# The norm of the heads: an inverse root with a Newton step instead of a root and a reciprocal

## The reference

```python
mu = jnp.mean(o, axis=-1, keepdims=True)                       # over the 64 channels of a head
var = jnp.mean(jnp.square(o - mu), axis=-1, keepdims=True)
o = (o - mu) * lax.rsqrt(var + GN_EPS) * lnx_w + lnx_b
bonus = sum over directions of (sum over channels of r * k_dir * r_k) * v
o = (o + bonus) * g                                            # g = sigmoid(gd) @ g_up
y_rwkv = o @ w_o_rwkv
```

## Time and profile before

| | |
|---|---|
| time, median of 3 runs | 2914.91 us (2911.87 to 2917.02) |
| the profiled execution's own time | 2906.37 us |
| its span | 2904.6 us |
| `head_norm`, first load to its last operation | about 1732 to 1806 us |
| TensorE, VectorE, ScalarE, GpSimd busy | 95%, 62%, 34%, 20% of the span |

### The profile page before, as it was taken

How to read it: one execution, slowest core, us unless ns; L and a number is a source line. 1 busy time by engine, 2 the same in 40 slices (tenths; PEclk the granted TensorE clock), 3 DMA queues, 4 the chain that set the end, 5 groups by cost and what they waited for, 6 DMA issues and landing times. The chain is left out here.

```text
span 2904.6 us, 58716 instructions
## 1 busy us (share of the span) xinstructions
PE 2760.1 (95%) x23048; PEld 2632.4 (91%) x23048; DVE 1799.9 (62%) x3391; ACT 995.6 (34%) x1768; POOL 575.7 (20%) x721
## 2 busy tenths in 40 slices
PE   7999999999999999999799987999899999999998
PEld 4999999999998999999788865799899999899998
DVE  4455565556636446434477858454777777777776
ACT  4211111111114323443266645212444443443442
POOL 4112233333203101222243314122300000100000
PEclk9999999999999999999899998999999999999999
DMA  6225556665511433344744423321243443344442
GB/s 277 66 79 142 153 154 166 173 157 147 141 40 72 142 126 113 140 167 174 211 104 112 108 63 144 127 78 62 94 128 126 136 134 123 110 131 135 137 134 94
DMA packets 246581, 371.75 MB, mean 128 GB/s; under 512 B 106528, under 2 KB 145824, under 8 KB 244032
## 3 DMA queue, kind: packets, MB, share of 16 engines
q1 hardware_dynamic: 213952, 295.45, 31.0%
q0 software_dynamic: 30208, 73.62, 10.3%
q10 hardware_dynamic: 2240, 0.13, 0.0%
HBM read 314.00 MB, written 101.25 MB: 143 GB/s over the span
## 5 line engine op out<-in xcount | busy, mean ns | idle before, releaser
L1788 PE MATMUL bank<-right_hi_ffn,left_lo_ffn 128*128 128x288 f32 x1240 | 368.4, 297 | 16.4 <-DVE u_ffn L1566 5.2
L1788 PE MATMUL bank<-right_lo_ffn,left_hi_ffn 128*128 128x288 f32 x1240 | 366.8, 296 | 0.0
L1788 PE MATMUL bank<-right_hi_ffn,left_hi_ffn 128*128 128x288 f32 x1240 | 365.8, 295 | 0.0
L917 DVE SCALAR_TENSOR_TENSOR x<-bank,gate,x 128x128 f32<-128x128 f32 (+1 forms) x480 | 235.9, 514 | 114.1 <-PE bank L1047 113.6
L2532 PE MATMUL bank<-h_hi_mix,wlo_in 128*128 128x384 f32 x840 | 288.6, 344 | 1.8 <-DVE h_lo_mix L242 1.8
L2532 PE MATMUL bank<-h_lo_mix,whi_in 128*128 128x384 f32 x840 | 282.5, 336 | 0.0
L2532 PE MATMUL bank<-h_hi_mix,whi_in 128*128 128x384 f32 x840 | 282.4, 336 | 0.0
L1353 ACT ACTIVATE left_hi_ffn<-raw_ffn 128x512 fp32r<-128x512 f32 x302 | 188.1, 626 | 225.3 <-PE bank L1788 219.2
L1546 DVE SCALAR_TENSOR_TENSOR x<-bank,gate,x 128x288 f32<-128x288 f32 (+2 forms) x440 | 190.1, 452 | 110.5 <-PE bank L1823 108.7
L1788 PEld LDWEIGHTS bank<-right_hi_ffn,left_lo_ffn 128*128 128x128 f32 x1240 | 234.3, 189 | 18.9 <-issue 17.7
L1102 ACT ACTIVATE act_out_ffn<-bank 128x384 f32<-128x384 f32 x66 | 32.4, 491 | 623.8 <-PE bank L1018 623.8
(11 more groups left out here) (357 smaller groups left out, 6893.6 us busy)
## 6 DMA issues: line engine op xcount, KB each, us to landing
raw_ffn<-tile_sums SPq DMA_DIRECT2D x168, 256.0 KB, 2.7
raw_ffn<-in_ffn_w SPq DMA_DIRECT2D x134, 256.0 KB, 2.9
raw_d_ffn<-in_ffn_w SPq DMA_DIRECT2D x66, 512.0 KB, 4.8
tile_sums<-in_ffn_w POOLq DMA_DIRECT2D x132, 256.0 KB, 7.1
ada_beside_ffn<-in_ada_w POOLq DMA_DIRECT2D x96, 256.0 KB, 3.5
raw_in<-in_w_in SPq DMA_DIRECT2D x35, 512.0 KB, 5.0
mix<-row_out SPq DMA_DIRECT2D x23, 576.0 KB, 3.2
raw_a_ffn<-in_ffn_w SPq DMA_DIRECT2D x22, 512.0 KB, 5.8
```

The lines of the kernel that those rows point to most:

```text
L917: ins = nc.vector.scalar_tensor_tensor(xs, kit.banks[4 + d % 4][:, a:b], kit.gate[:, gate, d, cond:cond + 1], xs, ALU.mult, ALU.add)
L1788: mm = nc.tensor.matmul(out, w[:, j, cols], v[:, r, k], start=(opens and a == 0 and k == 0 and m == 0), stop=(a == len(terms) - 1 and k == ...
```

## The change

The root becomes an inverse root (`Abs_reciprocal_sqrt`) on ScalarE, which also squares it. VectorE then does one Newton step in three products instead of a reciprocal and a product: with y the inverse root and V the sum of squares, (V + 64 eps) * y^2, minus 3*64, times y, and that times the centered tile and lnx_w * (-0.5/64), which is computed once. lnx_b is added in the product with the gate, since the gate's product is where the whole sum is multiplied. Squares and roots get two small buffers of their own (two slots each) instead of `hn_r`, so `square` no longer waits for `weighted`. TensorE's order becomes variance (1), sums (0), bonus (1), gate (2), channels (4); ScalarE's root (1), square (0), channels and high (4); VectorE's center (0), normed (1), bonus (1), gated (3); GpSimd's weighted (0), with_bonus (4), low (5).

```diff
         def tensor(pe):
             def sums(m):
                 if m >= 2:
-                    pe.wait_ge(s["rooted"], m - 1)
+                    pe.wait_ge(s["stepped"], m - 1)
...
-                nc.tensor.matmul(bank(m, 0), cst.pair_ones, at(r, m), start=True, stop=True).then_inc(s["var_done"], 1)
+                nc.tensor.matmul(bank(m, 0), cst.pair_ones, square_at(m), start=True, stop=True).then_inc(s["var_done"], 1)
...
-            skewed([(0, sums), (1, bonus), (1, variance), (2, gate), (3, channels)])
+            skewed([(1, variance), (0, sums), (1, bonus), (2, gate), (4, channels)])
...
                 act.wait_ge(s["centered"], m + 1)
-                act.wait_ge(s["rk_ready"], m + 1)
-                nc.scalar.activation(at(r, m), at(o, m), ACT.Square).then_inc(s["squared"], 1)
+                nc.scalar.activation(square_at(m), at(o, m), ACT.Square).then_inc(s["squared"], 1)
...
-                nc.scalar.activation(at(r, m), bank(m, 0), ACT.Sqrt, scale=1.0 / HD, bias=kit.eps[:, 1:2])\
-                    .then_inc(s["rooted"], 1)
-
-            def affine(m):
-                act.wait_ge(s["scaled"], m + 1)
-                nc.scalar.activation(at(r, m), at(o, m), ACT.Identity, scale=kit.col("lnx_w", ct_of(m)),
-                                     bias=kit.col("lnx_b", ct_of(m))).then_inc(s["affine"], 1)
+                nc.scalar.activation(root_at(m), bank(m, 0), ACT.Abs_reciprocal_sqrt, scale=1.0 / HD,
+                                     bias=kit.eps[:, 1:2]).then_inc(s["rooted"], 1)
+                act.wait_ge(s["rooted"], m + 1)
+                nc.scalar.activation(square_at(m), root_at(m), ACT.Square).then_inc(s["root_squared"], 1)
...
-            skewed([(0, square), (1, root), (2, affine), (3, channels), (3, high)])
+            skewed([(1, root), (0, square), (4, channels), (4, high)])
...
-                dve.wait_ge(s["rooted"], m + 1)
-                nc.vector.reciprocal(at(kd_sum, m), at(r, m)).then_inc(s["inverted"], 1)
+                dve.wait_ge(s["root_squared"], m + 1)
+                nc.vector.scalar_tensor_tensor(square_at(m), bank(m, 0), HD * GN_EPS, square_at(m), ALU.add, ALU.mult)\
+                    .then_inc(s["stepped"], 1)
+                dve.wait_ge(s["stepped"], m + 1)
+                nc.vector.scalar_tensor_tensor(root_at(m), square_at(m), 3.0 * HD, root_at(m), ALU.subtract, ALU.mult)\
+                    .then_inc(s["inverted"], 1)
                 dve.wait_ge(s["inverted"], m + 1)
-                nc.vector.tensor_tensor(at(o, m), at(o, m), at(kd_sum, m), ALU.mult).then_inc(s["scaled"], 1)
+                nc.vector.scalar_tensor_tensor(at(o, m), at(o, m), scale[:, ct_of(m):ct_of(m) + 1], root_at(m), ALU.mult, ALU.mult)\
+                    .then_inc(s["scaled"], 1)
...
-                nc.vector.tensor_tensor(at(o, m), bank(m, 2), at(v, m), ALU.mult).then_inc(s["gated"], 1)
-            skewed([(0, center), (2, bonus), (3, gated), (1, normed)])
+                nc.vector.scalar_tensor_tensor(at(o, m), at(v, m), kit.col("lnx_b", ct_of(m)), bank(m, 2), ALU.add, ALU.mult)\
+                    .then_inc(s["gated"], 1)
+            nc.vector.tensor_scalar(scale[:], kit.col("lnx_w", 0, CT), -0.5 / HD, None, ALU.mult).then_inc(s["weights"], 1)
+            skewed([(0, center), (1, normed), (1, bonus), (3, gated)])
...
-                pool.wait_ge(s["affine"], m + 1)
+                pool.wait_ge(s["scaled"], m + 1)
...
-                nc.gpsimd.tensor_tensor(at(v, m), at(v, m), at(r, m), ALU.add).then_inc(s["with_bonus"], 1)
+                nc.gpsimd.tensor_tensor(at(v, m), at(v, m), at(o, m), ALU.add).then_inc(s["with_bonus"], 1)
...
-            skewed([(0, weighted), (2, with_bonus), (3, low)])
+            skewed([(0, weighted), (4, with_bonus), (5, low)])
```

More of the change, by code:

```diff
@@ L3188, in head_norm @@
     s = {q: kit.sem("hn_" + q) for q in (
-        "loaded", "mean_done", "centered", "rk_ones", "rk_ready", "squared", "var_done", "rooted", "inverted", "scaled",
-        "affine", "bonus_done", "bonus_v", "with_bonus", "gate_done", "gated", "hi_ready", "lo_ready",
+        "loaded", "mean_done", "centered", "rk_ones", "rk_ready", "squared", "var_done", "rooted", "root_squared",
+        "stepped", "inverted", "scaled", "weights", "bonus_done", "bonus_v", "with_bonus", "gate_done", "gated", "hi_ready", "lo_ready",
         "f_in", "dft_in", "g_done", "g_ready")}
@@ L3199, in head_norm @@
         f, cs = buf("fo_f", [P, FG, T]), buf("fo_cs", [P, 2 * FD])
-        one_root = buf("hn_one_root", [P, 1])
+        one_root, scale = buf("hn_one_root", [P, 1]), buf("hn_scale", [P, CT])
+        squares, roots = buf("hn_squares", [P, 2, CH]), buf("hn_roots", [P, 2, CH])
         steps = CT * NC
@@ L3203, in head_norm @@
         at = lambda a, m: a[:, ct_of(m), part(m)]
+        square_at, root_at = (lambda m: squares[:, m % 2]), (lambda m: roots[:, m % 2])
         bank = lambda m, q: kit.banks[4 * (m % 2) + q][:, 0:CH]
@@ L3316, in channels @@
                 ins.then_inc(s["g_ready"], 1)
-            nc.scalar.activation(one_root[:], kit.eps[:, 0:1], ACT.Sqrt)
-            skewed([(0, square), (1, root), (2, affine), (3, channels), (3, high)])
+            nc.scalar.activation(one_root[:], kit.eps[:, 0:1], ACT.Abs_reciprocal_sqrt)
+            skewed([(1, root), (0, square), (4, channels), (4, high)])
         def vector(dve):
@@ L3327, in normed @@
             def normed(m):
[L3328 to L3329 removed]
+                dve.wait_ge(s["root_squared"], m + 1)
[4 more added lines that the diff above has]
+                    .then_inc(s["inverted"], 1)
                 dve.wait_ge(s["inverted"], m + 1)
[L3331 removed]
+                if m == 0:
+                    dve.wait_ge(s["weights"], 1)
+                nc.vector.scalar_tensor_tensor(at(o, m), at(o, m), scale[:, ct_of(m):ct_of(m) + 1], root_at(m), ALU.mult, ALU.mult)\
+                    .then_inc(s["scaled"], 1)
             def bonus(m):
@@ L3423, in tensor @@
                 if q < 3:
-                    pe.wait_ge(prev.s[("rooted", "bonus_v", "gated")[q]], prev.steps)
+                    pe.wait_ge(prev.s[("stepped", "bonus_v", "gated")[q]], prev.steps)
                 for i in range(4):
```

## The result

The changed kernel took 2893.4 us in the median of 6 runs (2887.14 to 2901.43), the kernel before 2913.39 (6 runs, 2908.27 to 2917.02): ratio 0.994, 95% interval 0.9926 to 0.9954, that is 13 to 22 us less, 17.5 in the middle (the two medians lie 20.0 apart). Timed again on another occasion it gave 0.9941 (0.9927 to 0.9955). The forecast was 2899.8, a gain of 15.1, with 2891 to 2908 as its range.

The account below looks back on a forecast made before the run. The prediction took VectorE, with its long reciprocal, to bound the stage at 5.5 us per tile. Start and period -15.3, tail +0.95 and clock -0.8 gave -15.1 us: 2899.8 from the median 2914.91, range 2891 to 2908.

Parts of the forecast that it names:

- VectorE's round and the port: VectorE's work per tile 3.13 us instead of 5.50; with port waits behind GpSimd, period 4.0, bounds 3.75 and 5.0.
- Rival 1: Both new VectorE products always wait a whole GpSimd product: period 5.0, gain 8.6, 2906.3 us; chance 17%.
- TensorE's floor of 3.75: TensorE's own work per tile in the stage, 3.75 us, taken as the shortest possible period.
- the second loop of the prediction: Loop from center through high and GpSimd's low, weighted and with_bonus to gated: 6.6 to 8.1 us for two periods.
- The start: DMA of `f` stays the wait; center(5) at 1753.7, then six periods of 4.0: center(11) 15.3 us earlier.
- The tail: From center(11) to the context transform, later lags of channels and low cost 0.95 us.
- The clock: TensorE's context transform runs at full clock: -0.8 us; the extra columns behind it taken as 0.
- Rival 4: TensorE's clock holds through the extra columns too: up to 5 us more gain, 2895; chance 11%.
- The table: ScalarE's next-stage Sqrt at 2056.83 will need a table load: 0, at most 1.3 us.
- rival 2: Inverse root and Square lie in different ScalarE tables, two loads per tile: gain about 7, 2908 us; chance 4%.
- Rival 3: TensorE's clock halves in the stage and stays there: 7.3 us per round, +5, 2920 us; chance 3%.
- The sum: Start and period -15.3, tail +0.95, clock -0.8: -15.1 us in all, giving 2899.8 us.

Follow-up runs that it names:

- e4: The changed kernel with the results of stepped and inverted written to PSUM instead of SBUF; median 2890.34 us, 0.9934 of the kernel before.
- e3: The changed kernel with GpSimd's with_bonus at lag 2 and low at 3 instead of 4 and 5; one execution 2905.57 us, kernel before beside it 2913.30.
- e2: The kernel before with the new order of all engines but the old arithmetic; one execution 2904.13 us, kernel before beside it 2913.30.
- e9: e4 with the 16 context transform products put among the 32 products of 2 columns; one execution 2890.72 us, kernel before beside it 2902.64.
- e6: The kernel before with idle matrix products in two holes of TensorE's tail; one execution 2910.45 us, kernel before beside it 2914.30.
- e8: The changed kernel with GpSimd's with_bonus at lag 2 and low at 4; one execution 2885.75 us, kernel before beside it 2902.64.
- e5: The changed kernel with TensorE's context transform made to wait for GpSimd's last product; one execution 2905.19 us, kernel before beside it 2914.30.

## Why the prediction was right, step by step

- **VectorE's round and the port**: 3.13 us plus waits, period 4.0; measured 3.96, and `inverted` and `scaled` 0.21 us each over their length in e4, 0.42 in all against 0.3 taken. The forecast had `inverted` alone wait; in the trace it differs from tile to tile, and `scaled` is held whole (1.24 against 0.62) in four of twelve. Rival 1 (always both, period 5.0) did not come. The port is shown by e4, which also shows TensorE's floor of 3.75, the lower bound of the range, to be too high (3.6). The reasoning behind it was incomplete: the rounds between GpSimd and ScalarE were taken as slack, and e3 shows that with low at lag 3 they alone make 6.2; the second loop of the prediction (6.6 to 8.1 for two periods) was the right kind of loop.
- **The start**: center 5 expected 21.7 us after the load, measured 20.1 and 21.7. The forecast said that the DMA stays the wait: so it was in the second profile (2.32 us), not in the first. The term was -15.3 for center 11, measured -17.2.
- **The tail**: +0.95 expected, +0.51 measured. The Fourier copies of ScalarE start 13.1 us after center 11, 13.4 expected; their cover held, with 0.4 us to spare (e4 above): the prediction had 12.0 us from the transform to the first large product, and 8.4 were left.
- **The clock**: the mis-sized term. -0.8 was taken for the transform alone, 0 for the columns, with half of 9 us as the bound, and the group was not considered. Measured: transform -0.95, columns -2.5, group -1.2, together -4.7. Rival 4 came true in part. Of the 6.2 us by which the stage's gain exceeds the forecast, 3.9 are this, 1.9 the start and period, 0.4 the tail.
- **The table**: as predicted, one load more at the next stage's Sqrt, and free. The timelines of ScalarE and VectorE in the changed kernel, against the earlier trace rows:

```profile
2044.70 1.67 ACT L1353 ACTIVATE left_hi_ffn<-raw_ffn 128x512 fp32r<-128x512 f32 x3 [3.38 <-DMA raw_ffn<-in_ffn_w]
2046.39 1.28 ACT L1265 ACT_TABLE_LOAD   x1
2047.68 0.50 ACT L1265 ACTIVATE inv_rms_ffn<-bank,eps 128x288 f32<-128x288 f32 x1
```

```profile
2048.23 1.94 DVE L1270 RECIPROCAL inv_rms_ffn<-inv_rms_ffn 128x288 f32<-128x288 f32 x1
```

  The rest of the span behind the stage is no longer with the load (1075.6 to 1081.1) than without it (1078.7 to 1080.4). Root and square stand in one table: no load lies between them (rival 2 fell). The Trainium skill, "ScalarE: Activation LUTs", section "What ACT_TABLE_LOAD costs", counts a drain of 1.38 us to each switch; here the load starts 0.02 us after the activation before it and the next activation 1.29 after the load's start, so no such drain shows, and the 1.29 stands.
- **Rival 3** (half clock in the stage): the clock was 1.00 in every window from 1752 to 1800.
- **The sum**: -15.1 forecast, -17.5 by the time, -21.3 and -19.8 by the stage in two profiles. Time and stage agree within their scatter. The median of 2893.4 lies in the full range but under the forecast's own 2896 to 2903 and under rival 4's 2895: the mechanism of the stage is as predicted, its gain is larger than the sum, mainly by the clock. That the time's 17.5 came within 2.4 us of the forecast gain is in part luck: the stage gained 4.7 to 6.2 us more than forecast, and the two medians lie 20.0 apart.

## What to carry to other kernels

When one long instruction is taken out of a software pipeline, list the loops through the in-order queues, with the number of rounds each spans: a lag of one round less on GpSimd cost 17 us here, and left it idle 44% of the time from center 5 to center 11 (11% in the changed kernel). An intermediate that two VectorE products pass on is better kept in PSUM than in SBUF while GpSimd is busy. Price TensorE's idle holes together with the clock of what follows them: filling two of them with products that compute nothing took 6 us out of the next 21. When a stage gets shorter, look again at what its cover was: here ScalarE's copies and VectorE's low parts were 0.4 us from holding up TensorE.

## What was not expected of the hardware

- The one that comes second at the port waits, whichever engine it is: VectorE's product 1.38 before, GpSimd's `low` 1.40 in e2.
- The clock falls during products of 2 columns though TensorE shows 2.00 of 2.00 us busy: in the changed kernel it was 1.00 over 1798 to 1800, 0.81 in the next window and then 0.50. A product of 128 columns after every second one did not hold it (e9). In e3 and e6 it was still 1.00 at the end of the columns (5.07 and 5.06 us) and fell as the large group began (0.58 and 0.50 in the 2 us there).
- After the fall the large Fourier products run at the lower level for a while: in e8 the columns are over 1.25 us sooner than in the changed kernel (5.33), but 13 large products instead of 6 follow the one before by 0.43 us instead of 0.23, and the group takes 9.23 instead of 7.94. So a clock held longer through the columns was paid back whole behind them there.
- TensorE's clock stood at 1.00 over 2 us in which it did nothing at all (e5, 1798 to 1800), and averaged 0.65 over the next 2.
